# An up projection in four groups of seven half-size products, and a scan's preparation moved into other stages

## The chip, the cores and the metric

The kernel runs on one core of one Trainium2 chip. The metric is the device time of one execution in microseconds (us); the figure for a kernel is the median of several runs. TensorE (PE in the rows; PEld is its weight load) multiplies matrices, VectorE (DVE) and ScalarE (ACT) work elementwise, GpSimd (POOL) fills and copies buffers here and issues some DMA transfers, and SyncE (SP) issues the transfers of the weights. All data are float32.

## The reference

Two layers act on 256 rows of width 1024, one after the other. The first is a hybrid of latent attention, gated linear attention and attention over a memory, then an output projection and a feed-forward block; the second holds a state space branch and a dilated attention. What the change touches is the end of the first layer, and the parameters of the second layer's state space branch:

```python
x = x + y @ w_o                                        # y: gated sum of three branches, w_o: 1024 x 1024
h2 = rms_norm(x, g_ffn)
return x + jnp.square(jax.nn.relu(h2 @ w_up)) @ w_down # w_up: 1024 x 4096, w_down: 4096 x 1024

# second layer, s5_branch: 64 groups of 64 states; C, B, lam and dt are parameters
mag = jnp.exp(lr * dt); ab_re = mag * jnp.cos(li * dt); ab_im = mag * jnp.sin(li * dt)
f_re = (nr * lr + ab_im * li) / den; f_im = (ab_im * lr - nr * li) / den     # nr = ab_re - 1
```

The scan over positions is done by rotating each state by its angle times the position. For that the kernel makes a table of cosines and sines for 128 steps by repeated doubling (`cs`), the parameters per lane (`lane`), C times f (`cc`) and the step times B (`bexp`, transposed into `bt`). None of this depends on x.

## The kernel before

The rows of x stand normalised and transposed in `hT` (128 channels of a block on the partitions, 8 blocks, 256 rows). The weights are streamed through a ring of three slots of 2 MB each, issued by SP in the order of `STREAMED`; a slot is filled again when TensorE is done with the job that held it. A *job* is one such slot: 1024 x 512 weights (or 512 x 1024) times 256 rows. TensorE accumulates it in one of two PSUM pairs, `pair0` and `pair1`, of 1024 columns each, used in turn; the next job but one waits until its pair has been taken out. Two banks, `turned`, are for transposes (ScalarE copies them out), and two, `score`, for attention. A float32 multiply is two passes of TensorE in the profile, a transpose is one.

Three projections of the first layer, the groups g0 to g2, are computed by Strassen's scheme in Winograd's form: the rows are cut into four blocks (two halves of the rows, two halves of the 1024 inputs), the weights of two slots (x and y, 512 inputs each, 1024 outputs) into four blocks, and seven products of half size stand for eight. VectorE makes the sums: T1 to T4 of weights (`group_t1` to `group_t4`, 128 x 2048 each, T4 over the weights in the ring), S1 to S4 of rows (`group_rows`, once for each `hT`), and puts the results together (`group_z`, `group_middle`, `group_last`: five operations of 128 x 512). ScalarE copies products 1 and 5 and takes out the first block. Product 5 needs T1 and S1, product 7 T3 and S3, product 3 S4, product 6 T2, product 4 T4 and Z. The order of the products is 1, 5, 2, 7, 3, 6, 4. The down projection uses the same scheme within each of its eight groups of 512 inputs (`mix` on VectorE, `multiply` on TensorE); its seven products are summed over the groups in seven PSUM banks, and x gets them at the end. `mix(g)` uses one of two buffers, so it waits for group g-2 of TensorE.

The order of the work is written out by hand, as one queue for each engine; semaphores join them (`link` and `mark` let an engine wait for its own instruction too, `step` doesn't). Around the change the queues before are:

- TensorE: gate2 and gate3, the output projection (wo0, wo1, by halves of the rows) with the transposes of y and of x between its parts; up0 and up1 by halves of the rows; the transposes of the lane parameters; up2, up3, the transposes of C (four banks), up4, up5, those of B (eight banks), up6, the product of B and C (`m0`), up7; then down.
- VectorE: the gated sum (`y_rows`); the residual and the normalisation of each half of the rows (`residual_norm`); the lane parameters (32 x 128 operations, `theta`, `lane_rows`); the step times B (`ab_ready`); the tables (`tables`), doubling n = 1 to 64; C times f (`c_ready`), that times the step (`ca_ready`); the squares of the feed-forward (`ff`), then `mix(0)` to `mix(7)` and the results.
- ScalarE: sigmoids of the gates, squares for the norms (`row_norm`), transposes out of PSUM (`turned`, `turned_rows`), exponential and sines of the lane parameters, and relu of each up job (`take`).
- GpSimd: the loads of the gates' biases; after the last residual a memset of `bexp`, nine loads of the parameters (`ssm_in`), and four copies that spread B.

## Time and profile before

| | |
|---|---|
| runs | 1007.48, 1009.59, 1009.45 us |
| median | 1009.45 us |
| the profiled execution | 1007.37 us, of which the span of instructions is 1005.6 us |
| granted clock of TensorE | 1.00 of 2.4 GHz |
| busy | TensorE 987.0 us, VectorE 558.9 us, ScalarE 202.8 us, GpSimd 25.9 us |
| moved by DMA | 139.69 MB, 139 GB/s on average |

Times in the rows are microseconds from the start of the span. A row of a timeline gives the start, the busy time, engine, line, operation, the tiles written and read, the shape, how many instructions are merged, and in brackets the idle time before it and what ended it. A duration of merged rows includes the short gaps between them. `arena` is the large buffer in which nearly all tiles lie, so tiles are told apart by line, shape and time.

### The profile page before, as it was taken

How to read it: one execution, taken by the hardware profiler on the slowest of the kernel's cores; microseconds unless marked ns; L12 is line 12 of the kernel's file. 1: busy time of each engine (PE TensorE's matmuls, PEld its weight loads, DVE VectorE, ACT ScalarE, POOL GpSimd, SP SyncE). 2: the span in 40 equal slices, each digit the busy share in tenths (PEclk: the TensorE clock that was granted, in tenths of full speed). 3: DMA queues.
4: the chain of work that ended last, by engine and by line, in shares of the span. 5: the costliest groups of instructions: out<-in, count | busy, mean ns of one | idle time of the engine just before them, and what ended most of it. 6: DMA issues, size and time to landing. Idle time of an engine off the chain costs nothing.

```text
span 1005.6 us, 11494 instructions
## 1 busy us (share of the span) xinstructions
PE 987.0 (98%) x4676; PEld 595.1 (59%) x4676; DVE 558.9 (56%) x1125; ACT 202.8 (20%) x405; POOL 25.9 (3%) x39
## 2 busy tenths in 40 slices
PE   6999899999999999999999999999999999999998
PEld 4944345755555459888744469458744444568443
DVE  5765941255677724799665552888966651332211
ACT  4313312223231113112000011001113121353000
POOL 3000000000000005000000000000000000000000
PEclk9999999999999999999999999999999999999999
DMA  9451731433244436634354443333244344211721
GB/s 324 136 188 57 257 125 42 168 124 128 84 135 159 139 113 183 215 101 152 135 187 181 167 147 136 138 123 129 85 167 150 105 164 167 84 42 43 250 84 42
DMA packets 63636, 139.69 MB, mean 139 GB/s; under 512 B 2864, under 2 KB 6208, under 8 KB 63584
## 3 DMA queue, kind: packets, MB, share of 16 engines
q1 hardware_dynamic: 61664, 134.56, 38.9%
q0 software_dynamic: 1712, 4.32, 1.8%
q8 instruction: 37, 0.61, 0.3%
q14 instruction: 15, 0.12, 0.0%
q10 hardware_dynamic: 208, 0.08, 0.0%
HBM read 137.90 MB, written 1.05 MB: 138 GB/s over the span
## 4 chain that ended last, share of the span: by engine, by line
PE 94%; DVE 4%; ACT 1%; DMA 0%; issue 0%; DVEq 0%; ACTq 0%
PE pair L1586 67%; PE pair L1894 5%; PE pair L1673 4%; PE turned L1527 4%; PE score L1894 3%; PE pair L1669 2%; DVE arena L791 2%; PE turned L1894 1%; PE score L2041 1%; PE score L1985 1%; PE score L2054 1%; PE score L1753 1%; PE score L1802 1%; PE score L1752 1%; PE score L1818 1%; PE turned L1972 0%
## 5 line engine op out<-in xcount | busy, mean ns | idle before, releaser
L1586 PE MATMUL pair<-ring,hT 128*128 128x512 f32 (+2 forms) x896 | 385.4, 584 | 0.0
L1586 PEld LDWEIGHTS pair<-ring,hT 128*128 128x128 f32 x896 | 167.0, 191 | 184.2 <-issue 180.1
L791 DVE TENSOR_TENSOR arena<-arena 128x256 f32<-128x256 f32 (+8 forms) x342 | 217.5, 652 | 76.8 <-PE score L1894 29.9
L1586 PE MATMUL pair<-hT,ring 128*128 128x256 f32 (+2 forms) x1104 | 189.0, 332 | 0.2 <-ACT hT L520 0.2
L1586 PEld LDWEIGHTS pair<-hT,ring 128*128 128x128 f32 (+1 forms) x1104 | 167.5, 190 | 19.3 <-issue 1.7
L1586 PE MATMUL pair<-ring,arena 128*128 128x512 f32 (+1 forms) x224 | 90.6, 562 | 0.0
L1022 DVE CUSTOM_DVE_ANT_0 arena<-score,masks 128x256 f32<-128x256 f32 (+2 forms) x40 | 18.1, 451 | 105.1 <-PE score L1753 46.6
L1586 PEld LDWEIGHTS pair<-ring,arena 128*128 128x128 f32 x224 | 42.1, 190 | 44.3 <-issue 43.5
L481 ACT ACTIVATE arena<-pair 128x512 f32<-128x512 f32 (+2 forms) x58 | 32.1, 573 | 179.3 <-PE pair L1586 179.2
L491 ACT ACTIVATE arena<-turned 128x512 f32<-128x512 f32 (+2 forms) x66 | 32.7, 536 | 133.4 <-PE turned L1527 133.4
L1527 PEld LDWEIGHTS turned<-ident,arena 128*128 128x128 f32 (+1 forms) x363 | 42.3, 144 | 27.7 <-issue 13.6
L1527 PE MATMUL turned<-ident,arena 128*128 128x128 f32 (+1 forms) x363 | 52.0, 283 | 6.6 <-DVE arena L817 2.1
L791 DVE TENSOR_TENSOR arena<-pair,arena 128x512 f32<-128x512 f32 x29 | 20.1, 692 | 44.2 <-PE pair L1586 37.6
L1894 PE MATMUL pair<-ring,arena 128*128 128x512 f32 x96 | 43.5, 592 | 0.0
L791 DVE TENSOR_TENSOR arena<-score,arena 128x512 f32<-128x512 f32 (+1 forms) x42 | 24.9, 624 | 21.6 <-PE score L2054 9.3
L791 DVE TENSOR_TENSOR arena<-ring 128x1024 f32<-128x1024 f32 (+1 forms) x22 | 33.3, 1516 | 3.9 <-DMA ring<-in_w_in 3.2
L791 DVE TENSOR_TENSOR xres<-pair,xres 128x512 f32<-128x512 f32 x10 | 6.9, 692 | 45.0 <-PE pair L1586 44.2
L1894 PEld LDWEIGHTS pair<-ring,arena 128*128 128x128 f32 x96 | 18.2, 190 | 23.0 <-issue 22.7
L604 ACT ACTIVATE arena<-arena,stats 128x256 f32<-128x256 f32 (+3 forms) x40 | 23.3, 584 | 41.0 <-DVE stats L1027 39.8
L1586 PE MATMUL pair<-arena,ring 128*128 128x256 f32 x128 | 29.8, 383 | 0.0
L1894 PE MATMUL score<-arena 128*128 128x512 f32 x64 | 29.8, 592 | 0.0
L505 ACT ACTIVATE arena<-xres 128x1024 f32<-128x1024 f32 x6 | 6.3, 1058 | 96.7 <-DVE xres L791 96.2
(212 smaller groups left out, 756.4 us busy)
## 6 DMA issues: line engine op xcount, KB each, us to landing
ring<-in_w_in SPq DMA_DIRECT2D x33, 2048.0 KB, 8.4
ring<-in_w_up SPq DMA_DIRECT2D x8, 2048.0 KB, 9.2
ring<-in_w_down SPq DMA_DIRECT2D x8, 2048.0 KB, 7.8
ring<-in_w_o SPq DMA_DIRECT2D x4, 2048.0 KB, 8.0
ring<-in_w_mem_kv SPq DMA_DIRECT2D x2, 2048.0 KB, 7.7
ring<-in_w_glu SPq DMA_DIRECT2D x2, 2048.0 KB, 7.8
ring<-in_w_ssm_out SPq DMA_DIRECT2D x2, 2048.0 KB, 8.0
ring<-in_w_ukv SPq DMA_DIRECT2D x4, 512.0 KB, 4.0
```

Of the source, the lines that this page charges most:

```text
L481: ins = act.activation(dst(t), p[:, 512 * t:512 * t + cols], func, scale=scale)
L491: act.activation(dst, src, ACT.Copy).then_inc(sem("turned_taken"), 1)
L604: ins = act.activation(s[:, half + a:half + a + w], s[:, half + a:half + a + w], ACT.Exp, bias=st[:, 340 + 2 * (n % 4) + t:341 + 2 * (n % ...
L791: return dve.tensor_tensor(o, a, b, op)
L1022: ins = dve.tensor_tensor_reduce(dst, src, mask, scale, -3e38, ALU.add, ALU.max, st[:, a:a + 1])
L1527: ins = pe.transpose(b[0:x.shape[1], a:a + rows], x, ident[0:rows, 0:rows])
L1586: ins = pe.matmul(o_, s, m, start=a, stop=b)
L1669: ins = pe.matmul(h[bank_][:, P * c:P * c + P], weights[:, k, P * c:P * c + P], rows[:, k, :], start=not onto and c == 0 and k == 0, stop= ...
L1673: ins = pe.matmul(h[bank_], rows[:, k, :], weights[:, k, :], start=not onto and k == 0, stop=k == 3, skip_group_check=True)
L1752: pe.matmul(o, qnT[:, SEQ * h + P * t:SEQ * h + P * t + P], knT[:, SEQ * h:SEQ * h + w], start=True, stop=False)
L1753: ins = pe.matmul(o, qpT[r, SEQ * (h // 2) + P * t:SEQ * (h // 2) + P * t + P], kpeT[r, 0:w], start=False, stop=True)
L1894: ins = pe.matmul(product[q], rows[:, k, :], weights[:, k, :], start=g == 0 and k == 0, stop=g == 7 and k == 1, skip_group_check=True)
```

## The change

Up projection: the eight jobs become four groups, g3 to g6 (`UP` = 3), each of two slots with 512 inputs and 1024 outputs, computed with the seven products of the groups. The first of them uses the order 1, 2, 5, 7, 3, 6, 4. The squares of the feed-forward move from VectorE to ScalarE, block by block (`square_first`, `square_rest`). The group's buffers lie where the tables will be (`cs`).

Scan preparation: its loads start when the last attention score has been taken (`SCORES`), before the gated sum; GpSimd also zeroes `cc` then (VectorE did), and `bexp` when the gated linear attention's output is done. The lane parameters are computed before the residuals of the first half of the rows, the step times B before those of the second; the transposes of the lane parameters and half of those of C go into the output projection, the rest into the first group of up. C times f is computed in the first group of up, C times the step in the second, B is transposed in the second, the product of B and C is made in the third, `mix(0)` in the fourth.

Tables: they are computed between the sums `mix(1)` to `mix(7)` of the down projection, with scratch space in `hT`; the last doubling is in four pieces.

```diff
-T_LANE = 44
-T_C = T_LANE + 4
-T_B = T_C + 8
+T_LANE = 40
+T_C = T_LANE + 6
+T_X = T_C + 2
+T_B = T_X + 8
+SCORES = 37
+UP = 3
...
-    out += [(f"up{i}", f"up{i}", "w_up", 0, DM, 512 * i, 512) for i in range(8)]
+    for i in range(4):
+        out += halves(UP + i, DM * i, "w_up")
...
+ORDERS = {i: (1, 2, 5, 7, 3, 6, 4) if i == UP else (1, 5, 2, 7, 3, 6, 4) for i in range(UP + 4)}
...
@@ GpSimd
-            pool.wait_ge(sem("residual"), taken("wo1")[1])
+            pool.wait_ge(sem("score_taken"), SCORES)
             bx = bexp.rearrange("p (i j s c) -> p i j s c", i=2, j=ST, s=2)
-            link(pool.memset(bexp, 0.0))
...
+            pool.memset(cc, 0.0).then_inc(sem("c_zero"), 1)
+            pool.wait_ge(sem("mixer_out"), 1)
+            link(pool.memset(bexp, 0.0))
             pool.wait_ge(sem("ssm_in"), 16 * 9)
...
@@ ScalarE
+            def square_first(i):
+
+                group_first(i, quarter_of_hidden(i, 0))
+                act.wait_ge(sem("group_act"), 3 * i + 3)
+                act.activation(quarter_of_hidden(i, 0), quarter_of_hidden(i, 0), ACT.Square).then_inc(sem("ff_ready"), 1)
+
+            def square_rest(i):
+
+                for n, name in ((1, "first_out"), (3, "second_out"), (2, "last_out")):
+                    x = quarter_of_hidden(i, n)
+                    act.wait_ge(sem(name), i + 1)
+                    link(act.activation(x, x, ACT.Relu))
+                    act.activation(x, x, ACT.Square).then_inc(sem("ff_ready"), 1)
...
-            for i in range(8):
-                take(f"up{i}", lambda t: hup[:, 1024 * i + 512 * t:1024 * i + 512 * t + 512], func=ACT.Relu)
...
+            turned_rows(1, hT)
+
+            act.wait_ge(sem("residual"), 2)
+            row_norm(0, xres[:, 0, :], 0, "x", hup[:, 0:1024])
+            turned(lane[:, 0:160], 160)
+            for k in range(2):
+                turned(c_turned[:, 512 * k:512 * k + 512], 512)
+            turned_rows(0, hT, "g_ffn")
+            act.wait_ge(sem("residual"), 4)
+            row_norm(1, xres[:, 1, :], 0, "x", hup[:, 0:1024])
+            group_copy(UP, 1)
+            for k in range(2, 4):
+                turned(c_turned[:, 512 * k:512 * k + 512], 512)
+            turned_rows(1, hT, "g_ffn")
+            group_copy(UP, 5)
+            square_first(UP)
+            square_rest(UP)
+            for i in range(UP + 1, UP + 4):
+                group_copy(i, 1)
+                group_copy(i, 5)
+                if i == UP + 1:
                     for k in range(8):
                         turned(bt[:, 512 * k:512 * k + 512], 512)
+                square_first(i)
+                square_rest(i)
...
@@ VectorE
             link(dve.reciprocal(den, den))
+            mark(residual("wo0", 0, 0), "residual")
             dve.wait_ge(sem("trig"), 1)
...
             mark(tt(fim, fim, den, ALU.mult), "lane_rows")
+            mark(residual("wo1", 1, 0), "residual")
+            row_norm(0, xres[:, 0, :], xn2[:, 0:DM], 0, "x")
+
             dve.wait_ge(sem("turned_taken"), T_LANE)
...
+            step_times_b(0)
+            step_times_b(1)
+            mark(residual("wo0", 0, 1), "residual")
+            group_t1(UP)
+            mark(residual("wo1", 1, 1), "residual")
+            row_norm(1, xres[:, 1, :], xn2[:, DM:2 * DM], 0, "x")
...
+            dve.wait_ge(sem("turned_taken"), T_X)
+            _, (a11, a12, a21, a22), _, (s1, s2, s3, s4), _ = group(UP)
+            mark(tt(s1, a21, a22, ALU.subtract), "group_rows")
+            mark(tt(s3, a11, a21, ALU.subtract), "group_rows")
+            group_t3(UP)
+            link(tt(s2, s3, a22, ALU.add))
+            mark(tt(s4, a12, s2, ALU.subtract), "group_rows")
...
-            for i in range(7):
-                ff(i)
-            dve.wait_ge(sem("m0_ready"), 1)
-            mark(dve.tensor_copy(m0, m0_bank[:, 0:256]), "m0_taken")
-            dve.wait_ge(sem("turned_taken"), T_B)
-            mix(0)
-            ff(7)
-            for g in range(1, 8):
-                mix(g)
+            for i in range(UP, UP + 4):
+                if i > UP:
+                    group_t3(i)
+                group_t2(i)
+                if i == UP:
+                    c_times_f()
+                if i == UP + 1:
+                    c_times_step()
+                if i == UP + 2:
+                    dve.wait_ge(sem("m0_ready"), 1)
+                    mark(dve.tensor_copy(m0, m0_bank[:, 0:256]), "m0_taken")
+                if i == UP + 3:
+                    dve.wait_ge(sem("turned_taken"), T_B)
+                    mix(0)
+                group_z(i)
+                group_t4(i)
+                group_middle(i, *hidden(i))
+                if i < UP + 3:
+                    group_t1(i + 1)
+                group_last(i, quarter_of_hidden(i, 2))
...
+            mix(1)
+            turns_begin()
+            for n in (1, 2, 4):
+                turns_real(n, every)
+                turns_imag(n, every)
+                square()
+            mix(2)
+            for n in (8, 16):
+                turns_real(n, every)
+                turns_imag(n, every)
+                square()
+            mix(3)
+            turns_real(32, every)
+            turns_imag(32, every)
+            square()
+            mix(4)
+            turns_real(64, low)
+            mix(5)
+            turns_imag(64, low)
+            mix(6)
+            turns_real(64, high)
+            mix(7)
+            turns_imag(64, high)
...
@@ TensorE
             half_job("wo0", 1)
+            R = srow[0:ST, :].rearrange("p (k n) -> p k n", n=128)
+            pe.wait_ge(sem("lane_rows"), 1)
+            turn("lane", [R[:, k, :] for k in (4, 5, 3, 7, 8)])
...
+            for m in range(2):
+                turn_c(m)
             half_job("wo1", 1, 0, 2)
             pe.wait_ge(sem("x_rows"), 3)
             turn_rows("x", xn2, 0)
             half_job("wo1", 1, 1, 2)
             is_turned("x")
...
+            group_multiply(UP, 1, True)
+            for m in range(2, 4):
+                turn_c(m)
+            assert n_unit["turned"] == T_C, n_unit
             pe.wait_ge(sem("x_rows"), 4)
             turn_rows("x", xn2, 1)
...
+            group_multiply(UP, 2, True)
+            group_multiply(UP, 5, True)
+            for q in (7, 3, 6, 4):
+                group_multiply(UP, q, True)
+            group_multiply(UP + 1, 1, True)
+            group_multiply(UP + 1, 5, True)
+            pe.wait_ge(sem("ab_ready"), 2)
+            pe.wait_ge(sem("c_ready"), 4)
+            for k in range(8):
+                turn("b", [bexp[:, 512 * k + P * m:512 * k + P * m + P] for m in range(4)])
+            assert n_unit["turned"] == T_B, n_unit
+            for q in (2, 7, 3, 6, 4):
+                group_multiply(UP + 1, q, True)
+            group_multiply(UP + 2, 1, True)
...
```

## Rows read from the trace of the kernel before

**Rows 1.** The page, part 1: busy us, share of the span, instructions of each engine.

```profile
PE 987.0 (98%) x4676; PEld 595.1 (59%) x4676; DVE 558.9 (56%) x1125; ACT 202.8 (20%) x405; POOL 25.9 (3%) x39
```

**Rows 2.** The page, part 4: the chain that ended last, by engine.

```profile
PE 94%; DVE 4%; ACT 1%; DMA 0%; issue 0%; DVEq 0%; ACTq 0%
```

**Rows 3.** Timeline of TensorE, up projection: start us, busy us, engine, line, operation, tiles.

```profile
375.66 7.31 PE L1586 MATMUL pair<-hT,ring 128*128 128x128 f32 x64
...
383.68 21.60 PE L1586 MATMUL pair<-hT,ring 128*128 128x128 f32 x192
...
435.68 27.79 PE L1586 MATMUL pair<-hT,ring 128*128 128x256 f32 x128
...
468.34 13.98 PE L1586 MATMUL pair<-hT,ring 128*128 128x256 f32 x64
...
497.57 1.88 PE L1894 MATMUL turned<-ring,arena 128*128 128x512 f32 x4
```

**Rows 4.** Chain of the work that ended last: start us, us; four products of group g0.

```profile
35.84 14.29 PE pair L1669 x128
```

**Rows 5.** Timeline of VectorE, group g0: a sum of weights, and Z out of PSUM.

```profile
18.01 2.29 DVE L791 TENSOR_TENSOR arena<-ring 128x2048 f32<-128x2048 f32 x1
...
39.51 0.69 DVE L791 TENSOR_TENSOR arena<-arena,pair 128x512 f32<-128x512 f32 x1 [1.53 <-PE pair L1669]
```

**Rows 6.** Timeline of VectorE during up: step times B, tables, C times f.

```profile
406.70 7.95 DVE L791 TENSOR_TENSOR arena<-arena 128x32 f32<-128x32 f32 x9 [3.40 <-ACT arena L491]
414.75 0.09 DVE L1262 MEMSET arena<- 128x32 f32 x1
...
441.25 13.90 DVE L791 TENSOR_TENSOR arena<-arena 128x32 f32<-128x32 f32 x7
...
459.58 6.20 DVE L791 TENSOR_TENSOR arena<-arena 128x1024 f32<-128x1024 f32 x6
465.81 1.41 DVE L1297 SCALAR_TENSOR_TENSOR arena<-arena 64x512 f32<-64x512 f32 x2
```

**Rows 7.** Timeline of VectorE: the last sums of the down projection, then its first result.

```profile
569.94 1.68 DVE L791 TENSOR_TENSOR arena<-arena 128x256 f32<-128x256 f32 x4 [5.31 <-PE score L1894]
...
575.44 1.22 DVE L791 TENSOR_TENSOR arena<-arena,ring 128x1024 f32<-128x1024 f32 x1
580.24 0.69 DVE L1339 COPY hT<-turned 128x512 f32<-128x512 f32 x1 [3.58 <-PE turned L1894]
```

**Rows 8.** Timeline of VectorE: end of down, the first tile is scaled.

```profile
591.22 0.75 DVE L817 TENSOR_SCALAR arena<-xres,stats 128x1024 f32<-128x1024 f32 x1
```

**Rows 9.** Timelines of VectorE, TensorE, ScalarE: gated sum and output projection.

```profile
338.74 2.87 DVE L791 TENSOR_TENSOR arena<-arena 128x512 f32<-128x512 f32 x4
...
342.13 1.04 PE L1527 MATMUL turned<-ident,arena 128*128 128x128 f32 x8
...
347.42 2.87 DVE L791 TENSOR_TENSOR arena<-arena 128x512 f32<-128x512 f32 x4
...
375.93 0.69 DVE L791 TENSOR_TENSOR xres<-pair,xres 128x512 f32<-128x512 f32 x1 [7.05 <-PE pair L1586]
...
380.04 0.75 DVE L817 TENSOR_SCALAR arena<-xres,stats 128x1024 f32<-128x1024 f32 x1
...
383.50 2.18 ACT L520 ACTIVATE hT<-turned,pcol 128x128 f32<-128x128 f32 x8 [5.69 <-PE turned L1527]
```

**Rows 10.** Timelines of GpSimd and VectorE: last bias load, memset, copies, VectorE beside them.

```profile
320.81 0.54 POOL L437 DMA_DIRECT2D arena<-in_b_gate  x1 [8.99 <-DVE arena L791]
376.68 3.52 POOL L443 MEMSET arena<- 128x4096 f32 x1 [55.34 <-DVE xres L791]
...
392.86 2.62 POOL L458 COPY arena<-arena 64x512 f32<-64x512 f32 x4 [3.95 <-DMA arena<-in_log_dt]
393.16 1.11 DVE L791 TENSOR_TENSOR arena<-arena 32x128 f32<-32x128 f32 x2 [12.37 <-ACT arena L673]
...
399.95 0.59 DVE L791 TENSOR_TENSOR arena<-arena 32x128 f32<-32x128 f32 x2 [0.49 <-ACT arena L677]
```

More of the change, by code:

```diff
@@ L186 @@
     "theta": "angle and log of the modulus", "trig": "ScalarE: cosine, sine and modulus", "lane_rows": "lane parameters",
-    "ab_ready": "halves of the step times B", "tables": "rotation tables, and C zeroed",
+    "ab_ready": "halves of the step times B", "mixer_out": "gated linear attention's output, normalised", "c_zero": "GpSimd: C zeroed",
     "c_ready": "quarters of C times f", "ca_ready": "halves of that times the step",
@@ L347, in build @@
         m0_bank = bank["score"][0]
[L348 removed]
+        first, second = (pair[OUTS.index(f"g{UP + 3}{x}") % 2] for x in "ab")
         product = {1: bank["turned"][0][:, :], 2: first[:, 0:512], 3: first[:, 512:1024], 4: bank["score"][1][:, :], 5: second[:, 0:512],
```

289 lines of the change are left out of this document (143 added, 146 removed).

## The prediction

> **What bounds the kernel now.** I read the page from the top. TensorE is busy for 987.0 of 1005.6 us [rows 1], and it carries 94% of the chain that ended last, VectorE 4% [rows 2]. So time is saved only by shortening TensorE's own work, and it is lost wherever another engine comes to be waited for. Next I read the timelines of TensorE and VectorE over the stages that are touched. The up projection runs from 375.66 to 497.57 us, nearly without a gap; the down projection follows it [rows 3]. VectorE, beside it, has room: it computes the tables during up, and in down it waits for TensorE before each group's sums (5.31 us idle in the row shown; five rows are like it) [rows 7].
>
> **What TensorE saves in up.** Before, two jobs run as four half-jobs of 128 columns: 21.60 us for three, 7.2 each, 28.8 for four. Six full jobs: 27.6 us for two, 82.9 for six. Sum 111.7 us [rows 3]. After, there are 4 x 7 = 28 products, each 16 matrix multiplies of 128 columns in two passes. The kernel already has exactly this form in its first group: 14.29 us for four products, 3.57 each [rows 4]. 28 x 3.57 = 100.0 us, so 11.7 us less. That the narrower multiplies lose their halving to weight loads is excluded by that row (111.6 ns a pass, against 216 ns for one of 256 columns). The transposes (rows of x, lane parameters, C, B) and the B times C product are the same in number: two banks of transposes take 0.87 us, all of B 4.9 us from the end of a job (463.4) to the next (468.34) [rows 3]. Lane and half of C (1.5 us) now stand inside the output projection, so up can begin at 377.2 instead of 375.66.
>
> **What VectorE must do in up, and where TensorE waits.** A weight sum of 128x2048 takes 2.29 us (2.32 with the gap behind it), an operation of 128x512 takes 0.69 (0.72) [rows 5]. A group is 4 x 2.32 + 5 x 0.72 = 12.9 us of VectorE against 25.0 us of TensorE, so a steady group has room; ScalarE has 9 instructions of some 0.6 us per group. The eight squarings of 1.25 us leave VectorE. The start is tight, because moved work stands in one queue there. I follow it.
> - VectorE ends the gated sum at 350.3 [rows 9]. The moved lane parameters took from 393.16 to 406.70 less 3.4 idle, 10.1 us, and some 1.3 of that was disturbance (below) [rows 6, 10]. So they are done near 360, before the residual that they are put ahead of (its half arrives at 361.0). TensorE asks for them at 367.9. Cost 0, slack about 8 us; if they were later than 361.3, the normalisation would move by as much. The nine loads are moved past 50 us of the GpSimd queue and land long before; SP's queue is not passed.
> - The lane bank is out of PSUM at 368.9. Then come three small products and the step times B, 8.05 us [rows 6], to 377.0, and only then the residual that frees the bank of product 1: 377.8. TensorE stands ready at 377.2. Wait 0.6.
> - Queued behind: the first weight sum, 2.32, to 380.1, the last residual, to 380.8, then square, root and scaling of the tile: 4.17 us from the end of the residual, as before [rows 9], to 385.0. TensorE has done product 1 (381.4) and two banks of C (382.3) by then. Wait 2.7.
> - Two banks of x, product 2, product 5 to 393.1; ScalarE has the tile out at 387.9 (2.18 us) [rows 9], so the row sums and T3 come in time (391.8, wanted at 393.1). Products 7, 3, 6 to 403.8. But VectorE does T2 (395.6), then C times f, 7.65 us [rows 6], then Z and T4: 406.4. Product 4 waits 2.6.
> - In the other groups the extra work (C times the step, 7.55 us; the copy of the B times C product; the first sums for down, 6.74 us) lies after T2 and ends before product 3 does, so T4 is ready about 1 us before its product. Cost 0; the 25.0 us of products hide it. Weights: a slot is freed after product 7 or 4, and transfers of 9 us have at least 9 us. Cost 0.
>
> Sum to the start of down: -11.7 for products, +5.9 of waits, -0.4 for the shorter waits at the transposes of C. That is -6.2: TensorE starts down at about 491.5 instead of 497.7. (The rows of TensorE start some 0.15 us before the row ahead of them ends, 497.57 here; I count from the ends.)
>
> **The down projection, where the gain goes.** TensorE needs 82.4 us to the end of product 1 of the last group. Before, the last sums were ready at 576.7, some 3.5 us ahead of that point (580.1) [rows 7]. After, VectorE starts at S + 0.95 (S is the start of down; one output out of PSUM) and has, ahead of the end of the last sums:
> - seven groups of sums of 6.74 us (569.94 to 576.66) [rows 7]: 47.2;
> - the tables up to the last doubling, 414.75 to 441.47 [rows 6]: 26.7;
> - three of the four pieces of the last doubling. This was six operations of 2.29 us [rows 6] and is now twelve of 1.23 + 0.03, 3.77 a piece: 11.3.
>
> None of the sums waits for TensorE any more, so it is one unbroken stretch: S + 86.15. TensorE wants it at S + 82.4. Wait 3.75. (On the way the fourth group's sums come about 1 us before their products; no wait.) Behind it the fourth piece, 3.77, and the nine operations of 0.72 that put the products together: S + 96.4. Then the same 4.17 us to the normalised tile: S + 100.6. TensorE ends its other products at S + 98.2 and waits 2.4 for that tile. Before, the tile came at 591.97 [rows 8], 94.2 after the start of down, when TensorE was just free. So down gives back 6.4 us: 491.5 + 100.6 = 592.1 against 592.0. Net +0.1 us. Behind it nothing is changed.
>
> **GpSimd beside VectorE in the output projection.** VectorE works without a pause up to 341.61, where the first tile of the gated sum is ready, and TensorE turns it from 342.3 [rows 9]: 0.6 us of slack. GpSimd now comes in there. Its last bias load is issued at 320.81 (0.54), then the nine loads (16.2 us from memset to copies, less 3.8 of memset, so to 333.8), two memsets of 3.5 to about 337.0, and the four copies, 2.62 us [rows 10], to 339.6. Beside the copies VectorE took 1.11 us for two operations of 32x128, against 0.59 for two such alone: half of the time is lost, near 1.3 us over 2.62 [rows 10]. I take half to all of that, less the slack: 0.5 us. The bounds are 0 (they fall on the additions out of PSUM at 337.3 to 338.7) and 2.0 (VectorE stands for all 2.62 us). The memset of before ran beside the small operations that end in the row of 380.04, and the 4.17 us of that chain are what it takes elsewhere [rows 9, 10]; I take 0 for memsets.
>
> The Trainium skill (SBUF — State Buffer, Who interferes with whom) says that a VectorE instruction with two SBUF inputs contends with a GpSimd instruction that reads SBUF, not with one that only writes it. The row of the copies agrees; no row here has a memset beside wide operations. By that rule the memsets are free, by the exclusive use that the page tells of two-port modes they would not be, which is the slower rival.
>
> **Sum.** +0.1 + 0.5 = +0.6 us on a span of 1005.6. The profiled execution took 1007.37 (1.8 around the span) and lies 2.1 below the median of 1009.45, whose runs are 1007.48, 1009.59 and 1009.45. I add the difference to the median: 1010.0.
>
> **Rivals.**
> - *VectorE stands beside GpSimd (slower).* Memsets and copies together are 9.6 us, all from 330 to 340, where VectorE has 0.6 us of slack. At the rate of the copies (half of their time) it loses 4.7 us and TensorE 4.1; net +4.2, 1013.6. For it: the copies did slow it. Against: the small operations beside the memset. It decides from 0.6 us of loss. Chance 0.18. The queues at the start of up being late by more than I followed goes the same way, +2 to +3, chance 0.07.
> - *VectorE is not last in down, or waits in up are smaller (faster).* If VectorE's stretch in down fitted into TensorE's time, all of -6.2 + 0.5 would stand: 1003.8. It needs 6 us less in 89 us of work whose lengths are known within about 0.5, so in full 0.05. A part of it gives -2 to -4, 1006.5: every microsecond of the 5.9 of waits in up that is not there moves S and all that hangs on it, and pieces shorter by 2 us together do the same behind S. Chance 0.12 more.
> - *The change doesn't do what it says.* If a product cost 4.0 us, a 28th of the old jobs, the halving would bring nothing; down starts 12 us later than in my sum and all behind it too: 1022. The first group's row speaks against it. Chance 0.02.
> - *Forecast*, within 2 us of before: 0.56.
>
> **How the numbers follow.** 0.2% is 2.0 us, about what a measurement of this kernel can tell from no change. Faster 0.17, same 0.56, slower 0.27. The range reaches from the partial gain, 1006, to the contention, 1014.
>
> **What would show it.** Right: products of 3.57 us; TensorE waits near 377, 382 and 404 (0.6, 2.7, 2.6), down starts 6 us earlier, VectorE has no idle time between the first sums of down and its last product, TensorE waits 3.8 us before product 6 of the last group and 2.4 before it turns the tile, and the next projection starts at 595 as before. Wrong: VectorE idle in down (tables cheaper), operations longer than 1.24 us there, or a gap of TensorE before 342 with stretched VectorE operations near 335.

## The result, and the profile after

The changed kernel takes 1012.09 us in the median of 19 runs (1009.25 to 1014.14), the kernel before on the same chip 1007.82 us in 19 runs (1006.99 to 1009.59). The ratio is 1.0036, 95% interval 1.0027 to 1.0044. So it is slower by some 3.6 us by that ratio, which compares means, and by 4.3 us by the medians. The prediction was +0.6, 1010.0 in all, and its likeliest case was a time within 2 us of before (0.56). The result lies inside its range, on the slower side (0.27), but by neither of the two slower rivals: the contention with GpSimd, on which the upper end of the range rests, did not come, and the waits in up were as long as foreseen. That the range holds the result is luck.

The page, part 1, and the chain by engine (parts 1 and 4, as [rows 1] and [rows 2]):

```profile
PE 981.4 (97%) x4932; PEld 596.3 (59%) x4932; DVE 598.8 (59%) x1162; ACT 218.1 (22%) x429; POOL 30.1 (3%) x40
...
PE 83%; DVE 15%; ACT 1%; issue 1%; DMA 0%; DVEq 0%; ACTq 0%
```

TensorE is busy 5.6 us less and the span, 1010.1 us, is 4.5 us longer: it is idle 10 us more. VectorE's part of the chain has grown from 4% to 15%. The up projection, timeline of TensorE (columns as in [rows 3]):

```profile
379.71 3.81 PE L1790 MATMUL pair<-hT,ring 128*128 128x128 f32 x32 [0.47 <-DVE xres L851]
383.36 1.04 PE L1648 MATMUL turned<-ident,arena 128*128 128x128 f32 x8
386.88 1.09 PE L1648 MATMUL turned<-ident,arena 128*128 128x128 f32 x8 [2.49 <-DVE arena L877]
...
391.39 7.31 PE L1790 MATMUL pair<-arena 128*128 128x128 f32 x64
398.53 3.74 PE L1790 MATMUL pair<-arena,ring 128*128 128x128 f32 x32
...
408.29 0.94 PE L1790 MATMUL pair<-hT,ring 128*128 128x128 f32 x6 [2.45 <-DVE ring L851]
...
445.66 1.48 PE L2012 MATMUL score<-arena 128*32 128x32 f32 x128
448.98 3.73 PE L1790 MATMUL pair<-arena 128*128 128x128 f32 x32 [1.84 <-issue]
```

The products cost 3.57 us each (391.39 to 398.53 for two). There are the three foreseen waits, 0.47, 2.49 and 2.45 us. And there is a gap of 1.84 us that was not foreseen: it stands behind the 128 small passes (64 multiplies) that make B times C, called the burst below, and the profile names no releaser for it, only "issue". The end of the down projection, TensorE and then VectorE:

```profile
581.47 3.78 PE L2025 MATMUL pair<-arena 128*128 128x512 f32 x4 [3.48 <-DVE arena L851]
585.05 6.47 PE L2025 MATMUL pair<-ring,arena 128*128 128x512 f32 x12
591.36 5.31 PE L2025 MATMUL score<-arena 128*128 128x512 f32 x12
596.55 1.09 PE L1648 MATMUL turned<-ident,arena 128*128 128x128 f32 x8
...
599.53 7.41 PE L1707 MATMUL pair<-hT,ring 128*128 128x128 f32 x64 [0.17 <-ACT hT L556]
```

```profile
574.70 1.68 DVE L851 TENSOR_TENSOR arena<-arena 128x256 f32<-128x256 f32 x4
576.41 1.23 DVE L851 TENSOR_TENSOR arena<-ring 128x1024 f32<-128x1024 f32 x1
...
580.19 1.22 DVE L851 TENSOR_TENSOR arena<-arena,ring 128x1024 f32<-128x1024 f32 x1
```

VectorE has no idle time in brackets here (compare [rows 7], 5.31 us idle before the same sums), and TensorE waits 3.48 us for them. But the four passes behind that wait take 3.78 us, and the next twelve 6.47, where four take 1.88 elsewhere in the same stage and twelve 5.31 in the next row. The granted clock says why (windows; the columns are stretch, length, busy time and instructions of PE, PEld, DVE, ACT and POOL, then PEclk, DMA share, GB/s):

```profile
581.00:586.00 5.00, 4.53 (x6) 1.95 (x7) 4.86 (x6) 0.00 (x0) 0.00 (x0) 0.50 0.01 3
```

After the wait TensorE ran at 0.50, that is 1.2 GHz instead of 2.4. The 16 passes took 10.05 us (581.47 to 591.52). Kernel 5 below has the same wait without a fall, and there they take 7.13 us (581.64 to 588.77), so the fall costs 2.9. (The 6.87 us in the expectation of kernel 1 is too low: it is four times the step of 1.72 us between such blocks in mid-stream.)

**Where the 4.5 us of the span come from.** Two places ahead of 340 us differ between the two profiled executions: the start of the program by some 0.85 us, and one more place (timeline of TensorE, first the kernel before, then after):

```profile
125.82 1.09 PE L1527 MATMUL turned<-ident,arena 128*128 128x128 f32 x8 [2.14 <-DVE arena L791]
127.25 1.24 PE L1527 MATMUL turned<-ident,arena 128*128 128x128 f32 x8 [0.34 <-ACT arena L495]
```

```profile
126.67 3.55 PE L1648 MATMUL turned<-ident,arena 128*128 128x128 f32 x15 [2.14 <-DVE arena L851]
```

Behind the same wait of 2.14 us the transposes ran slower in the execution of after (granted clock 0.95 over 100 to 135 us, 1.00 before). Both kernels do the same there. Together that makes 1.85 us ahead of 340 us: TensorE turns y at 343.98, against 342.13 [rows 9]. The gap behind B times C adds 1.84. The late clock fall costs 2.9, of which 1.7 would have been the wait for the tile, as kernel 5 shows; from the end of the wait of 3.48 us to the next projection the two differ by 1.1 us (18.06 against 16.97). Sum 1.85 + 1.84 + 1.1 = 4.8. The next projection starts at 599.53, 4.5 us later than before:

```profile
595.01 7.19 PE L1586 MATMUL pair<-hT,ring 128*128 128x128 f32 x62 [0.17 <-ACT hT L520]
```

So the rearranged schedule alone is worth some -0.3 us in this execution. The place of 340 us is no fixed mark: over the twelve profiled executions TensorE turns y between 341.61 and 344.48 us. Part of that is the same fall near 126 us, part is scatter at the start of the program, so single times and medians of few runs are uncertain by some 1 us.

### The profile page after: what moved, and what is told of

It is laid out like the page before. It is cut to its first block, busy times and chain, and to the rows that moved or that the text cites. A ratio compares the mean times of both kernels' runs of the same rounds, so it can differ in the third digit from the quotient of the medians.

```text
span 1010.1 us, 12115 instructions
## 1 busy us (share of the span) xinstructions
PE 981.4 (97%) x4932; PEld 596.3 (59%) x4932; DVE 598.8 (59%) x1162; ACT 218.1 (22%) x429; POOL 30.1 (3%) x40
## 4 chain that ended last, share of the span: by engine, by line
PE 83%; DVE 15%; ACT 1%; issue 1%; DMA 0%; DVEq 0%; ACTq 0%
PE pair L1707 55%; PE pair L1790 11%; DVE arena L851 9%; PE pair L1794 4%; PE turned L1648 4%; DVE hT L851 2%; DVE ring L851 1%; PE score L2176 1%; PE pair L2025 1%; PE score L2120 1%; PE score L2189 1%; PE score L1874 1%; PE score L1923 1%; PE score L1873 1%; PE score L1939 1%
## 5 line engine op out<-in xcount | busy, mean ns | idle before, releaser
L851 DVE TENSOR_TENSOR arena<-arena 128x256 f32<-128x256 f32 (+6 forms) x296 | 179.5, 621 | 24.7 <-ACT arena L517 13.7
L1707 PE MATMUL pair<-hT,ring 128*128 128x128 f32 (+2 forms) x464 | 76.4, 324 | 0.2 <-ACT hT L556 0.2
L1707 PEld LDWEIGHTS pair<-hT,ring 128*128 128x128 f32 (+1 forms) x464 | 66.0, 188 | 9.0 <-issue 1.3
L1790 PE MATMUL pair<-hT,ring 128*128 128x128 f32 x480 | 55.7, 275 | 2.9 <-DVE ring L851 2.5
L1790 PE MATMUL pair<-arena 128*128 128x128 f32 x480 | 55.9, 275 | 1.8 <-issue 1.8
L1790 PEld LDWEIGHTS pair<-hT,ring 128*128 128x128 f32 x480 | 54.6, 192 | 4.1 <-DVE ring L851 2.6
L1790 PEld LDWEIGHTS pair<-arena 128*128 128x128 f32 x480 | 54.8, 192 | 1.8 <-issue 1.7
L851 DVE TENSOR_TENSOR arena<-ring 128x1024 f32<-128x1024 f32 (+1 forms) x30 | 51.7, 1723 | 5.6 <-DMA ring<-in_w_in 4.6
L517 ACT ACTIVATE arena<-pair 128x512 f32<-128x512 f32 (+2 forms) x42 | 22.8, 566 | 98.7 <-PE pair L1707 98.6
L851 DVE TENSOR_TENSOR arena<-arena,ring 128x1024 f32<-128x1024 f32 (+1 forms) x15 | 25.8, 1723 | 14.0 <-PE pair L1790 13.6
```

The costliest lines, as they stand in the source:

```text
L517: ins = act.activation(dst(t), p[:, 512 * t:512 * t + cols], func, scale=scale)
L851: return dve.tensor_tensor(o, a, b, op)
L1707: ins = pe.matmul(o_, s, m, start=a, stop=b)
L1790: ins = pe.matmul(h[bank_][:, P * c:P * c + P], weights[:, k, P * c:P * c + P], rows[:, k, :], start=not onto and c == 0 and k == 0, stop= ...
```

## Experiments

Every execution has its own mean granted clock, over all kernels here from 0.992 to 1.000, and its time follows it, so times are compared below also at equal clock. The kernels were measured in three series, on three chips: kernels 1, 3, 5 and 6, then 2, 4, 9 and 10, then 7 and 8. Each ratio is to the kernel before in the same series (medians 1007.66, 1007.38 and 1007.65 us; one run of 3951 us in the first left out); differences to the changed kernel, 1012.09, go across series. Before: 16 of 19 runs of the second series have 1.000 (1006.6 to 1008.7 us), 3 have 0.998; in the other two 23 of 28 and 15 of 19 have 1.000. In the series of the result its clocks are not on record, but 9 of 19 runs lie at 1009.05 to 1009.59, where otherwise its runs of 0.998 lie. Changed: none of 19 has 1.000; 0.998 gives 1009.25, 0.995 some 1012, 0.993 some 1014.

**1. Keep TensorE busy in the two late waits.**

```diff
             multiply(1, 7).then_inc(sem("product"), 1)
+            (a11, _, _, _), (b11, _, _, _), _, _ = quarters(7)
+            for k in (0, 1, 0, 1):
+                pe.matmul(bank["turned"][1][:, :], a11[:, k, :], b11[:, k, :], start=True, stop=True)
...
             multiplied(multiply(4, 6), 6)
+            for k in (0, 1):
+                pe.matmul(bank["turned"][1][:, :], a11[:, k, :], b11[:, k, :], start=True, stop=True)
```

> The changed kernel with dummy multiplies of TensorE put into its two late waits of the down projection: four of 128x512 ahead of the wait for the last sums (3.4 us, the wait was 3.48), two ahead of the wait for the first tile (1.7 us). They go to a free bank of PSUM and nobody reads them. In the changed kernel the granted clock fell to 0.50 behind the wait of 3.48 us, and 16 passes took 10.05 us instead of 6.87. Theory (the wait itself costs a second time, through the clock): the clock stays at 1.00 to the end of down, the 16 passes take 6.87 us, the tile is ready some 0.9 us earlier, and the runs lie 1 to 3 us below those of the changed kernel (median 1012.1), so at 1009 to 1011, with a smaller spread. Rival (the clock falls for another reason, or its fall is hidden behind VectorE): granted clock again 0.50 there, or no change of the median beyond 0.5 us.

Measured: 1010.16 us (12 runs), ratio 1.0029 (1.0015 to 1.0043). In its profile the late fall is gone:

```profile
580.87 3.60 PE L2073 MATMUL turned<-ring,arena 128*128 128x512 f32 x8
584.51 1.98 PE L2025 MATMUL pair<-arena 128*128 128x512 f32 x4
586.33 5.31 PE L2025 MATMUL pair<-ring,arena 128*128 128x512 f32 x12
```

But this execution has falls at two other waits, at the start of up and before product 4 of the first group (granted clock 0.57 over 386 to 390 and over 410 to 414 us). The first:

```profile
386.51 1.97 PE L1648 MATMUL turned<-ident,arena 128*128 128x128 f32 x8 [2.50 <-DVE arena L877]
388.27 4.54 PE L1790 MATMUL pair<-hT,ring 128*128 128x128 f32 x32
```

It costs 1.6 us up to the next products (386.51 to 392.65, against 386.88 to 391.39 in the changed kernel). So the falls are not tied to one wait; which of them an execution has differs from one to the next. Six of the twelve runs have clock 1.000, with 1008.83 to 1009.38 us. That is what the schedule takes without any fall: still 1.6 us over before at clock 1.000 in the same series (1007.5). The median of after lies another 3 us higher (1012.1 less 1009.1). That is an estimate of all its falls together, the one near 126 us included, and of the scatter between series. The median fell as expected; the spread didn't shrink (1008.8 to 1014.5).

**2. All four longer waits filled.** As 1, with three more multiplies before the wait for the second tile of x and three before product 4 of the first group.

> The changed kernel with dummy multiplies in all four longer waits of TensorE: three of 128x512 (2.6 us) ahead of the wait for the second tile of x (2.49), three ahead of product 4 of the first group (2.45), and the six of the earlier fill in down. Nobody reads them. Earlier profiles show the granted clock at 0.93 over 376 to 425 us in four kernels that have these two waits, and 1.00 in others of the same waits: the fall comes in some executions only. Theory (waits of 2 to 3.5 us are where the clock falls, by chance): with them filled the clock stays at 1.00 in most executions, all but those that lose it near 126 us (0.998), and the median is 1009.0 to 1009.6, 3 us below the changed kernel; what is left above the kernel before is the 1.84 us gap behind the small multiplies. Rival (the clock falls for other reasons, such as the denser use of TensorE): spread and median as in the changed kernel, 1012.

Measured: 1008.13 us (10 runs), ratio 1.0007 (0.9998 to 1.0017). Five runs have clock 1.000: 1006.92 to 1007.59, median 1007.4, which is what before takes at 1.000. The multiplies shifted the instructions, and the gap behind B times C is gone in this kernel (446.18 us for the burst, 447.59 for what follows). No run is under 0.998, where 18 of 19 of the changed kernel are: with the waits filled the late falls are gone. So without falls and without the gap the change is worth nothing, as the sum said. At clock 1.000, this kernel and kernel 1 differ by 1.7 us, about the length of the gap.

**3. Two pieces of the table taken out of VectorE's stretch in down.**

```diff
             mix(6)
-            turns_real(64, high)
             mix(7)
-            turns_imag(64, high)
...
             row_norm(1, xres[:, 1, :], xn3[:, DM:2 * DM], 0, "x")
+            late_tmp = arena[:, work_at + 6144:work_at + 8192]
+            turns_real(64, high, late_tmp)
+            turns_imag(64, high, late_tmp)
```

> The changed kernel with the last two of the four pieces of the last doubling (twice 3.77 us of VectorE) moved behind the normalisation of the second tile, where VectorE has 19 us without work; their scratch space lies elsewhere. Theory (VectorE's stretch in down is what took back the gain): the sums of the last group end at S + 82.4 instead of S + 86.15, so the wait of 3.48 us goes, and the tile comes 7.5 us earlier on VectorE, bounded now by TensorE: the next projection starts 6 us earlier after the start of down (97.4 us instead of 103.9), the clock stays at 1.00, and the time is 1004 to 1006, 6 to 8 us below the changed kernel. Rival (something else holds the end of down, the products or the squares of ScalarE): under 2 us gained.

Measured: 1007.53 us (10 runs), ratio 0.9995 (0.9985 to 1.0004), 4.6 us less than the changed kernel. Both late waits are gone:

```profile
580.74 1.94 PE L2026 MATMUL pair<-arena 128*128 128x512 f32 x4
582.52 5.31 PE L2026 MATMUL pair<-ring,arena 128*128 128x512 f32 x12
587.67 5.31 PE L2026 MATMUL score<-arena 128*128 128x512 f32 x12
592.85 1.09 PE L1649 MATMUL turned<-ident,arena 128*128 128x128 f32 x8
```

At clock 0.998 this kernel takes 1005.8, at 0.995 1008.4, some 3.5 to 4 us under the changed kernel. In its profile the next projection starts 97.4 us after the start of down, as expected, instead of 104.0. So VectorE's unbroken stretch was what held TensorE in down. The time expected, 1004 to 1006, was missed by 1.5 us: the gap is still there (2.13 us), and the profiled execution has two falls in up (granted clock 0.93 over 376 to 425 us).

**4. VectorE's queue in up laid anew.** The residual goes ahead of the step times B, whose two halves move behind it; C times f and C times the step move by a group; B is transposed behind product 3 of the second group.

```diff
-            step_times_b(0)
-            step_times_b(1)
             mark(residual("wo0", 0, 1), "residual")
...
+            step_times_b(0)
             dve.wait_ge(sem("turned_taken"), T_X)
...
                 if i == UP:
-                    c_times_f()
+                    step_times_b(1)
                 if i == UP + 1:
-                    c_times_step()
+                    c_times_f()
                 if i == UP + 2:
+                    c_times_step()
```

> The changed kernel with VectorE's queue in up laid out anew: the step times B comes after the residuals and the second normalisation (first half) and after T2 of the first group (second half), C times f in the second group, C times the step in the third; TensorE transposes B behind product 3 of the second group. Theory (the three waits at the start of up, 5.4 us, come from work queued ahead of what TensorE waits for, and each us of them moves the start of down): the waits shrink to under 1 us in all, down starts 5 us earlier, the wait of 3.5 us in down stays as it is, and the time is 5 us below the changed kernel, 7 where the clock falls less: 1005 to 1007. Rival (the gain is given back in down, since VectorE is last there): down starts 5 us earlier and ends at the old time, 1012. VectorE's stretch in down begins with the start of down, so I hold this for unlikely.

Measured: 1006.23 us (10 runs), ratio 0.9983 (0.9972 to 0.9993). Of 5.4 us of waits at the start of up one is left:

```profile
384.05 1.09 PE L1648 MATMUL turned<-ident,arena 128*128 128x128 f32 x8 [0.58 <-DVE arena L877]
...
443.50 5.36 PE L1790 MATMUL pair<-arena 128*128 128x128 f32 x32 [1.92 <-issue]
```

The median gains 5.9 us on the changed kernel, within what was expected. The gap behind B times C is still there, and in this execution the passes behind it run slowly as well (5.36 for 3.73, granted clock 0.66 over 443 to 448), so the gap, too, can bring a clock fall.

**The gap behind B times C.** Its cause was open. Two kernels moved the burst against TensorE's products.

**5. The whole burst one product later.**

```diff
-            for j in range(ST):
...
-            for q in (5, 2, 7, 3, 6, 4):
+            group_multiply(UP + 2, 5, True)
+            b_times_c(range(ST))
+            for q in (2, 7, 3, 6, 4):
```

> The changed kernel with the product of B and C (64 small multiplies, 128 passes in 1.4 us) one product later in the third group of up, so about 3.6 us later, when the weight transfer that began at 442.2 is almost over. In the changed kernel TensorE had a gap of 1.84 us behind these multiplies that no semaphore explains. Theory 1 (the next instructions come by DMA and queue behind the weight transfer): the gap shrinks to under 0.5 us, time 1.5 us lower. Theory 2 (so many small instructions in 1.4 us outrun the fetching wherever they stand): the gap of 1.8 us moves with them. Theory 3 (an unseen wait for the sum that product 5 needs): the gap stays between products 1 and 5, or goes because product 5 comes earlier.

Measured: 1010.76 us (10 runs), ratio 1.0026 (1.0012 to 1.0040).

```profile
451.13 1.55 PE L2014 MATMUL score<-arena 128*32 128x32 f32 x128
452.62 3.62 PE L1790 MATMUL pair<-hT,ring 128*128 128x128 f32 x30
...
581.64 1.98 PE L2031 MATMUL pair<-arena 128*128 128x512 f32 x4 [3.47 <-DVE arena L851]
...
595.62 1.09 PE L1648 MATMUL turned<-ident,arena 128*128 128x128 f32 x8 [1.70 <-DVE arena L877]
```

No gap, as the first theory says and the second doesn't; the time fell by 1.3 us, foreseen were 1.5. In this execution the clock held behind the 3.47 us (it fell behind the two waits in up), and the second late wait of the prediction appears, 1.70 us for the tile.

**6. The burst in four parts,** each ahead of a product.

```diff
+            for n, q in enumerate((5, 2, 7, 3, 6, 4)):
+                if n < 4:
+                    b_times_c(range(8 * n, 8 * n + 8))
+                group_multiply(UP + 2, q, True)
```

> The changed kernel with the product of B and C cut into four parts of 16 small multiplies, one ahead of each of the products 5, 2, 7 and 3 of the third group. Theory 1 (the next instructions queue behind a weight transfer): a gap may stay, shorter, while that transfer runs, 0 to 1.8 us. Theory 2 (the burst outruns the fetching): no gap at all, each part 0.35 us, time 1.8 us lower than the changed kernel. Theory 3 (an unseen wait): the gap stays at 1.8 us before product 5.

Measured: 1011.85 us, only 4 runs (clock 0.995, 0.995, 0.995, 0.996), ratio 1.0035 (1.0021 to 1.0049). Each part takes 0.49 us and no gap stands behind any, not even before product 5, where the third theory had it stay. In the time this can't be seen: the runs are few and all have falls.

**7 and 8. What makes the gap.** Kernel 7 shifts TensorE's stream by twelve tiny multiplies, kernel 8 holds the transfer back. Two theories: the place of the burst against the fetches of TensorE's instructions (A), or the transfer of the weights of group g6, which SP issues at 442.19 and which is under way when the burst ends (B).

```diff
+            for k in range(12):
+                pe.matmul(bank["score"][1][:, 0:32], a11[:, k % 4, :], b11[:, k % 4, 0:32], start=True, stop=True)
             pe.wait_ge(sem("x_rows"), 4)
```

> The changed kernel with twelve multiplies of 32 columns, whose results nobody reads, put in front of TensorE's work on the second quarter of x, inside the 2.49 us that it waits there for VectorE. They shift every later instruction of TensorE by the same number of places in its stream and cost nothing in time. Theory A (the 1.84 us behind the 128 small multiplies of B and C comes because a fetch of TensorE's instructions falls behind that burst): the burst now lies elsewhere against the fetches, the gap is gone or moves by whole places, and the time is about 1.8 us under the changed kernel's at the same granted clock (about 1010.3 instead of 1012.1 at the median). Theory B (the transfer of the third group's weights, which is in flight at 442 to 450, holds up the fetch): the gap stays at 1.8 to 2.0 us, and the time stays at about 1012. The clock's falls at the waits are the same in both.

```diff
+                        if name == "g6x":
+                            sp.wait_ge(sem("group_product"), product_at(5, 2))
```

> The changed kernel with one edit: the transfer of the weights of one pair is issued only after the third product of the third group, so that it is not in flight while the 128 small multiplies of B and C run. TensorE's instruction stream is unchanged. Theory A (the place of the burst against the instruction fetches makes the gap): the gap of 1.8 us behind the burst stays, and the time stays at about 1012. Theory B (the weight transfer beside it makes the gap): the gap is gone, and the time falls by 1.8 us to about 1010.3. A third outcome, weights that come too late for their first product, would be a wait of TensorE on that transfer later in the up projection, of up to some us.

Measured: kernel 7 1008.40 us (10 runs), ratio 1.0003 (0.9993 to 1.0012); kernel 8 1008.29 us (10 runs), ratio 1.0019 (1.0001 to 1.0036). The gap is gone in both:

```profile
446.38 1.48 PE L2015 MATMUL score<-arena 128*32 128x32 f32 x128
447.79 3.84 PE L1790 MATMUL pair<-arena 128*128 128x128 f32 x32
```

```profile
443.82 1.48 PE L2014 MATMUL score<-arena 128*32 128x32 f32 x128
445.23 3.84 PE L1792 MATMUL pair<-arena 128*128 128x128 f32 x32
```

So each theory was right where it expected the gap to go and wrong where it expected it to stay: the gap needs both. Both times lie 3.7 to 3.8 us under the changed kernel, twice what was expected; the rest is fewer falls, and whether the missing gap or another chip makes them fewer isn't shown. Kernel 8 still has all four waits. Five of its ten runs take 1007.2 to 1007.6 us, as long as the kernel before, and three take 1012.6 to 1013.3. In its profile TensorE turns y at 342.12, so its times can be laid beside those of before and of the prediction as they stand:

```profile
491.78 1.88 PE L2027 MATMUL turned<-ring,arena 128*128 128x512 f32 x4
...
577.82 2.87 PE L2027 MATMUL pair<-arena 128*128 128x512 f32 x4 [3.47 <-DVE arena L853]
...
594.77 7.41 PE L1709 MATMUL pair<-hT,ring 128*128 128x128 f32 x64 [0.17 <-ACT hT L558]
```

The next projection starts 0.24 us earlier than before (595.01), though the clock fell behind the 3.47 us here too (0.66 over 578 to 583): this shorter fall went wholly into the wait for the tile.

The queue of instruction fetches shows how the two causes meet. It had 39 packets in the changed kernel, for 9864 passes and weight loads of TensorE, and 37 before, for 9352, one for some 253 both times; so I take them for TensorE's. The instruction packets (q8, some 16 KB each) of kernel 8, in the stretches 441.8 to 442.0 and 446.0 to 446.2 us (columns: packets, MB, share of 16 engines), and of the changed kernel in 442.2 to 446.6 and 446.6 to 446.8:

```profile
q8 instruction: 1, 0.02, 44.3%
...
q8 instruction: 1, 0.02, 42.1%
```

```profile
q1 hardware_dynamic: 280, 1.15, 75.9%
...
q1 hardware_dynamic: 18, 0.07, 91.3%
q8 instruction: 1, 0.02, 32.8%
```

TensorE's stream is the same in these two. Without the transfer a fetch comes 2.0 us ahead of the burst (441.8 against 443.82). In the changed kernel the same fetch would be due at 443.6; instead 280 packets of weights pass, and the fetch comes only at 446.6, 3 us late and 0.5 us before TensorE runs dry (447.14). It starts again at 448.98, 2.4 us after that packet. In kernel 7 a fetch comes between 441.8 and 442.0, ahead of the issue at 442.91, and the next between 449.4 and 449.6; in kernel 2, which has no gap either, one comes between 442.8 and 443.0, right behind the issue at 442.71. In kernels 1, 3 and 4, which all have the gap (1.98, 2.13, 1.92 us), the fetch comes 4.4 to 4.6 us after the issue of the transfer, as in the changed kernel (442.19 to 446.6). In kernel 5 it is late as well (449.8), but the burst starts only after it, at 451.13, and nothing is lost. At clock 0.998 the changed kernel takes 1009.25 in its only such run, kernels 7 and 8 1006.7 to 1007.6 in nine of ten (the tenth 1009.16).

The Trainium skill (Runtime: NRT & Kernel Launch, Instruction fetch mechanics) says that an engine fetches its instructions over a DMA queue of its own in blocks of 256, while it executes the block before, and calls the cost "mostly hidden". The packets here agree with the blocks (the burst and its weight loads are 256 instructions); the cost does not: 1.84 to 2.13 us in four traces in which the fetch stood behind the transfer, and the measurement decides.

**9 and 10. All of it together:** the queue of kernel 4, three pieces of the table late, and the burst one product later or in four parts.

> The three edits together: the new queue of VectorE in up, the product of B and C one product later, and three pieces of the last doubling (11.3 us) behind the second tile of the down projection. Theory (the change's 11.7 us of saved products are all to be had once nothing waits): TensorE has no wait above 0.7 us from 340 to 600, the next projection starts 11 to 12 us earlier than in the kernel before, the clock stays at 1.00 but for the fall near 126 us, and the time is 996 to 997.5 against 1007.5. Rival (VectorE is late with the tables for the first scan tile, since 11.3 us now stand in 16 to 19 us of free time): a wait of 1 to 3 us near 615 us, 998 to 1000.

> As the one before it, but the product of B and C cut into four parts ahead of products 5, 2, 7 and 3. Theory: the same within 0.5 us. If the gap behind the small multiplies depends on a weight transfer that happens to run, the two may differ by up to 1.8 us, since the group's place in time has moved.

Measured: 996.93 us (4 runs, 996.84 to 998.54), ratio 0.9897 (0.9882 to 0.9912), and 997.93 us (4 runs, 996.62 to 998.86), ratio 0.9902 (0.9887 to 0.9917). Both beat the kernel before by some 10 us, and the changed kernel by 14 to 15. The second, where y is turned, at the start of up and at the end of down:

```profile
341.61 1.09 PE L1649 MATMUL turned<-ident,arena 128*128 128x128 f32 x8
...
381.91 1.09 PE L1649 MATMUL turned<-ident,arena 128*128 128x128 f32 x8 [0.58 <-DVE arena L877]
...
581.24 1.09 PE L1649 MATMUL turned<-ident,arena 128*128 128x128 f32 x8
...
584.22 7.41 PE L1708 MATMUL pair<-hT,ring 128*128 128x128 f32 x64 [0.17 <-ACT hT L556]
```

The next projection starts at 584.22 instead of 595.01, 10.8 us earlier; 0.5 of it lies ahead of the change, since y is turned at 341.61 instead of 342.13. So 10.3 us of TensorE's saving of 11.7 (plus the 0.4 at the transposes of C) arrive. In kernel 9, with the burst in one piece, it is 11.1 (344.42 to 586.17, against 342.13 to 595.01 before). With four runs each, the two medians don't tell the kernels apart.

## Why the prediction was right or wrong, point by point

- **The saving on TensorE, 11.7 us: right.** 3.57 us a product, and kernel 9 shows that all but about 1 us of it can be had (11.1 of 12.1, the 0.4 at the transposes of C counted in).
- **The three waits in up: right in place and size.** Foreseen 0.6, 2.7 and 2.6, measured 0.47, 2.49 and 2.45. With 1.85 us taken off, they end at 377.86, 385.03 and 406.44, against 377.8, 385.0 and 406.4 in the sum. Following VectorE's queue instruction by instruction paid.
- **The start of down: the step failed.** Foreseen 491.5. Measured 495.43 plus 0.14 for the overlap of rows, less 1.85: 493.7. 1.84 of the 2.2 us between is the gap behind B times C, which the prediction counted as "the same in number". The multiplies were the same in number; what stood beside them, a transfer of weights issued 3.5 us ahead of the burst, was not. Kernel 8, without the gap, starts down at 491.78 plus 0.14, 491.9. The 0.4 us that are left were not looked for.
- **VectorE's stretch in down: right.** TensorE wants the last sums at S + 82.4 (S is the start of down; 577.99 less 495.57) and has them at S + 85.9; foreseen were 82.4 and 86.15, a wait of 3.75, measured 3.48. Kernel 3 shows that it is this stretch.
- **The wait for the tile, 2.4 us: right in kind, too large.** It is 1.70 in kernel 5: the tile is turned 13.98 us after the end of the wait for the last sums (581.64 to 595.62), foreseen were 14.45, and TensorE's products between take 12.3 instead of 12.05. In the changed kernel's profile it isn't seen at all, since the clock fall made TensorE itself late.
- **GpSimd in the output projection, +0.5 us: mis-sized, and the rival with it refuted.** Timelines of GpSimd and VectorE:

```profile
331.58 3.53 POOL L488 MEMSET arena<- 128x4096 f32 x1
335.02 3.53 POOL L490 MEMSET arena<- 128x4096 f32 x1
338.62 3.30 POOL L494 COPY arena<-arena 64x512 f32<-64x512 f32 x4
```

```profile
331.95 7.14 DVE L851 TENSOR_TENSOR arena<-arena 128x2048 f32<-128x2048 f32 x4
339.12 1.42 DVE L851 TENSOR_TENSOR arena<-pair,arena 128x512 f32<-128x512 f32 x2
340.58 3.33 DVE L851 TENSOR_TENSOR arena<-arena 128x512 f32<-128x512 f32 x4
```

  VectorE's four wide operations beside the two memsets take 7.14 us, and 7.14 us in the trace of before, where GpSimd stands still. The copies run from 338.62 to 341.92. The first 1.42 us of VectorE beside them are additions out of PSUM, which take 1.42 us before as well. The four operations of 128x512 behind those take 3.33 against 2.87 [rows 9], and the copies 3.30 against 2.62 [rows 10]. So VectorE lost 0.46 us in the 1.34 us in which both ran, a third and not half, and over half of the copies' time it lost nothing. The 0.6 us of slack took that up: TensorE turned y without a wait. By the rule of the Trainium skill (SBUF — State Buffer, Who interferes with whom) a GpSimd instruction that only writes doesn't disturb a VectorE instruction with two SBUF inputs, one that reads does; both rows agree.
- **What the prediction left out: what a wait does to TensorE's clock.** It priced a wait at its length. In the trace of the changed kernel the late fall cost 1.1 us beyond the waits and the one near 126 us some 1.0; a fall behind a wait in up costs 1.6 (kernel 1). For all falls together kernel 1 gives an estimate of 3 us in the median. The profile of before has nearly no wait of TensorE between 376 and 592 us (1.0 us in four), and most of its executions show clock 1.000; the change put three waits of 2.45 to 3.48 us, one of up to 1.70 and the gap of 1.84 into that stretch.
- **The sum.** Without gap and falls the arithmetic holds: +0.1 foreseen, 0 measured (kernel 2 at clock 1.000), -0.24 at the next projection in the trace of kernel 8. The gap, 1.8, and the falls, some 3 in the median by that estimate, are what was missing. The starting point hid a part: two of the three runs that the prediction started from, 1009.59 and 1009.45, lie where runs of clock 0.998 of the kernel before lie, and its median of 19 runs is 1007.82, 1.6 lower. So the time foreseen, 1010.0, is only 2.1 us under the 1012.09 measured, while the difference to before was missed by 3.7.

Still open: a fall between 100 and 135 us (granted clock 0.95 there) lies in code that the change doesn't touch, and yet it is in the profiles of the changed kernel and of kernels 2, 3, 4, 7 and 9, not in those of before and of kernels 1, 5, 6, 8 and 10. Kernels 2, 9 and 10, in whose traces no wait over 0.6 us is left between 340 and 592 us, have 0.998 in 10 of 18 runs, the kernel before in the same series in 3 of 19. That speaks for the change making this fall more frequent, but it wasn't tested. Nor was it tried to place a fetch against a transfer on purpose, beyond the cases above.

## What to carry to other kernels

A change that shortens TensorE's work and opens waits in exchange isn't even at equal time: each of the waits of 1.9 to 3.5 us here could cost the clock as well, from nothing, where a later wait took the fall up, to 1.6 us a time. So lay the other engines' queues anew with the change, so that moved work stands where it has slack; the same change was worth −10 us with three reorderings and +4 without. And look for an "issue" gap behind a long run of tiny TensorE instructions. Here the run began 3.5 us after a 2 MB transfer was issued, and the instruction fetch stood behind it; moving either one closed the gap.

## What the runs showed of the hardware

- TensorE's granted clock can fall to 0.50 (1.2 GHz) where it has stood for 1.9 to 3.5 us (1.92 in kernel 4, 3.48 in the changed kernel): four passes of 128x512 took 3.78 us instead of 1.98. The same wait brings it in one execution and not in another (3.48 us: fall in the changed kernel; 3.47 us: none in kernel 5).
- An instruction fetch of TensorE can wait behind the packets of a 2 MB transfer: 4.4 to 4.6 us from the issue of the transfer to the fetch, 3 us late by the comparison with kernel 8, and a stall of 1.8 to 2.1 us behind 128 small passes, which take 1.48 us in all.
- GpSimd's copies and VectorE's operations on two SBUF inputs slow each other: in 1.34 us of overlap the copies lost 0.68 us (3.30 for 2.62) and VectorE 0.46 (3.33 for 2.87); a memset of 128x4096 beside them costs neither anything that can be seen.
